# Attention by groups: V in high and low halves, two heads' turned probabilities split, scaled by GpSimd, query tile by query tile

## What is computed

```
g_logits                                   # 3 gates (sigmoid) per head
q: 16 heads of 64;  kc,vc, ks,vs, kw,vw: 4 groups of 64 (one group serves 4 heads)
p_c = masked_softmax(q . compress(kc) * scale)          # 31 compressed keys
o_c = p_c @ compress(vc)
o_s = masked_softmax(q . ks * scale, causal) @ vs        # 512 keys
o_w = masked_softmax(q . kw * scale, causal) @ vw        # 512 keys
o   = o_c * gates[0] + o_s * gates[1] + o_w * gates[2]
return o.reshape(S, 1024) @ w_out
```

## Time and profile before

| | |
|---|---|
| time, median of 3 runs | 1523.73 us (1522.63 to 1525.72) |
| profiled execution: time, span | 1524.09 us, 1522.3 us |
| busy: PE, PEld, DVE, ACT, POOL | 1468.9, 1221.6, 718.9, 716.8, 677.4 us |
| PE busy, share of the span | 96% |
| mean granted TensorE clock | 0.991 |
| attention groups of layer 1 | about 775 to 1050 us |

### The profile page before, as it was taken

One profiled execution on the slowest core, in us unless ns is written; L12 is line 12 of the kernel. 1 busy time (PEld: TensorE's weight loads), 2 busy tenths in 40 slices (PEclk: granted clock), 3 DMA queues, 4 the chain that ended last, 5 costly groups with the idle time before them and its releaser, 6 DMA issues.

```text
span 1522.3 us, 23455 instructions
## 1 busy us (share of the span) xinstructions
PE 1468.9 (96%) x7566; PEld 1221.6 (80%) x7566; DVE 718.9 (47%) x1256; ACT 716.8 (47%) x1305; POOL 677.4 (44%) x970
## 2 busy tenths in 40 slices
PE   6999978999999999999999999999999999999998
PEld 5877757888888888877978787878888888888886
DVE  5477772643434300246466767674644444410053
ACT  5245543654444423357365656464744444423262
POOL 4634434365656555364420202111465656555452
PEclk9999998999999999999999999999999999999999
DMA  5321111223232333242510101010132222332221
GB/s 201 121 70 56 55 42 56 94 100 106 87 106 87 106 102 97 70 135 84 167 44 15 56 1 55 14 41 21 66 136 96 96 96 96 96 97 98 97 97 56
DMA packets 37131, 126.22 MB, mean 83 GB/s; under 512 B 6096, under 2 KB 6864, under 8 KB 36816
## 3 DMA queue, kind: packets, MB, share of 16 engines
q1 hardware_dynamic: 31824, 115.88, 22.9%
q10 hardware_dynamic: 5248, 9.55, 1.8%
HBM read 123.32 MB, written 2.10 MB: 82 GB/s over the span
## 4 chain that ended last, share of the span: by engine, by line
PE 58%; issue 17%; POOL 16%; DVE 5%; ACT 4%; POOLq 0%; ACTq 0%; DVEq 0%
PE banks_a L1204 22%; POOL w_lo L297 15%; PE banks_b L1213 9%; PE banks_a L1213 8%; PE banks_a L1576 4%; PE banks_b L1204 4%; PE banks_a L1181 4%; PE banks_b L1548 2%; PE banks_b L1368 2%; DVE nm L940 1%; PE banks_a L1387 1%; PE banks_a L1467 1%; ACT w_hi L358 1%; ACT y L361 1%; PE banks_b L1551 0%
## 5 line engine op out<-in xcount | busy, mean ns | idle before, releaser
L297 POOL TENSOR_TENSOR w_lo<-w_raw,w_hi 128x256 fp32r<-128x256 f32 x852 | 648.0, 793 | 767.0 <-ACT w_hi L358 766.9
L358 ACT ACTIVATE w_hi<-w_raw 128x1024 fp32r<-128x1024 f32 x213 | 225.6, 1061 | 284.1 <-PE banks_b L1213 137.5
L1204 PE MATMUL banks_a<-nT_hi,w_hi 128*128 128x512 f32 (+1 forms) x968 | 344.5, 377 | 0.0
L1204 PE MATMUL banks_a<-nT_lo,w_hi 128*128 128x512 f32 (+1 forms) x968 | 342.7, 375 | 0.0
L1204 PE MATMUL banks_a<-nT_hi,w_lo 128*128 128x512 f32 (+1 forms) x968 | 342.2, 375 | 0.0
L1204 PEld LDWEIGHTS banks_a<-nT_hi,w_hi 128*128 128x128 f32 x968 | 174.6, 190 | 32.0
L1204 PEld LDWEIGHTS banks_a<-nT_hi,w_lo 128*128 128x128 f32 x968 | 173.7, 189 | 32.1
L1204 PEld LDWEIGHTS banks_a<-nT_lo,w_hi 128*128 128x128 f32 x968 | 173.8, 189 | 31.3
L846 DVE SCALAR_TENSOR_TENSOR y<-banks_a,conv,y 128x511 f32<-128x511 f32 x88 | 66.0, 750 | 218.2 <-ACT y L459 217.6
L459 ACT ACTIVATE y<-banks_a,conv 128x512 f32<-128x512 f32 x88 | 68.6, 780 | 207.6 <-PE banks_a L1204 207.5
L940 DVE TENSOR_REDUCE nm<-banks_b 128x2 f32<-128x256 f32 (+2 forms) x96 | 79.2, 825 | 27.1 <-PE banks_b L1371 14.5
(11 more groups left out here) (256 smaller groups left out, 2400.6 us busy)
## 6 DMA issues: line engine op xcount, KB each, us to landing
w_raw<-in_w SPq DMA_DIRECT2D x213, 512.0 KB, 3.3
g_pre<-in_gains ACTq DMA_DIRECT2D x6, 512.0 KB, 5.1
x<-in_x SPq DMA_DIRECT2D x4, 512.0 KB, 9.6
g_post<-in_gains ACTq DMA_DIRECT2D x4, 512.0 KB, 7.6
out<-x SPq DMA_DIRECT2D x4, 512.0 KB, 2.6
pe_raw<-in_pT ACTq DMA_DIRECT2D x2, 512.0 KB, 6.0
w1k<-in_w ACTq DMA_DIRECT2D x1, 1024.0 KB, 4.9
w1v<-in_w ACTq DMA_DIRECT2D x1, 1024.0 KB, 6.9
```

The lines of the kernel that those rows point to most:

```text
L297: pool.tensor_tensor(w_lo[slot][:, cols], w_raw[k % RAW][:, cols], w_hi[slot][:, cols].bitcast(F32), ALU.subtract).then_inc(S["w_lo_done"], 1)
L358: act.activation(w_hi[u % RING][:, :], w_raw[u % RAW][:, :], ACT.Copy).then_inc(S["w_hi_done"], 1)
L1204: m = pe.matmul(bank[:, cols], w[:, k * P:(k + 1) * P], r[:, k, cols], start=(k, pas) == (0, 0), stop=(k, pas) == (KT - 1, 2))
```

## The change

All of it lies in the groups of layer 1.

- **Steps.** `sequence` now runs over head pair m, tile k and branch c. A step holds one branch of two heads j, and steps 0 to 7 of a pair have 1, 1, 4, 4, 2, 2, 3, 3 key blocks. Scores, maxima, exponentials and transposes are as many and as wide as before.
- **Normalising and gates.** After the exponentials of a step VectorE clamps and inverts the row sums (`inverse_sums`), and GpSimd multiplies `gp` in place by the inverse and by the gate (`weigh`): two TENSOR_SCALARs a step. `gturn` waits for them.
- **Chunks.** Turned probabilities are handled in 12 chunks for each pair (24 in a group), of one or two key blocks of both heads, 256 or 512 columns. ScalarE copies a chunk to `gpT_hi`, then VectorE subtracts that into `gpT_lo`.
- **Values.** `Vs` holds V's high and low half side by side as the weights (128 columns); the turned probabilities stream, 256 columns at a time, in `float32r`. Two products for each key block, and the result comes out turned already, with the low half's product in rows 64 to 127. All branches accumulate in A[0] and A[1].
- **End of a pair.** ScalarE copies rows 64 to 127 out (`spill`), VectorE adds them (`fold`); `gturn_o`, `read_branches` and `add_branches` are gone. For the first pair this happens at step 9.
- **Compressed branch.** `Vc` replaces `Vblk`, its low half is made once and copied to three more row blocks; the compressed probabilities are normalised and gated before they are turned, split in high and low, and `cvalues` opens the accumulation (8 products for each pair). VectorE's `blocks_out` is gone.
- TensorE and GpSimd have the four groups written out instead of a loop; GpSimd's `low` of a group's fourth unit is spread behind steps 3 to 6.

```diff
+        sequence = [(m, c, k) for m in range(2) for k in range(TT) for c in range(2)]
+        chunks = [(n, kb, min(2, ORDER[k] + 1 - kb)) for n, (m, c, k) in enumerate(sequence)
+                  for kb in range(0, ORDER[k] + 1, 2)]
+        CHUNKS = len(chunks)
+        chunks_of = [[i for i in range(CHUNKS) if chunks[i][0] == n] for n in range(len(sequence))]
...
+            def weigh(g, n):
+
+                m, c, k = sequence[n]
+                qt = ORDER[k]
+                width = (qt + 1) * P
+                pool.wait_ge(S["gstat_done"], 16 * g + n + 1)
+                for j in range(2):
+                    cols = gp[:, n % DEEP, j, 0:width]
+                    gate = gates[:, qt, bass.ds(12 * g + (3 * (2 * m + j) + 1 + c), 1)]
+                    pool.tensor_scalar(cols, cols, grec[:, n % 4, j:j + 1], gate, ALU.mult, ALU.mult)\
+                        .then_inc(S["gnorm_done"], 1)
...
+                for n in range(len(sequence)):
+                    weigh(g, n)
+                    if 3 <= n < 3 + PARTS:
+                        low(UG + 3, (UG + 3) % RING, UG + 4 * i + 4, (n - 3,))
+            for g in range(GROUPS):
+                group(g, g)
...
+            act.wait_ge(S["vclo_done"], 1)
+            for h in range(1, GHEADS):
+                signal(act.activation(Vc[N_PAD * h:N_PAD * h + N_PAD, :, HEAD:2 * HEAD],
+                                      Vc[0:N_PAD, :, HEAD:2 * HEAD].bitcast(F32), ACT.Copy), "kvc_done", GHEADS + h)
...
+            def spill(pair):
+                act.wait_ge(S["gpv_done"], (CHUNKS // 2) * pair + CHUNKS // 2)
+                for j in range(2):
+                    signal(act.activation(of_half(oT[side(j), :]), of_head(side(1), j), ACT.Copy), "gspill_done",
+                           2 * pair + j + 1)
+
+            def goT_high(pair):
...
+                    signal(act.activation(gp[:, n % DEEP, j, 0:width], B[2 * (n % 2) + j][:, 0:width], ACT.Exp,
+                                          bias=nm[:, n % 4, j:j + 1], accum_out=gsum[:, n % 4, j:j + 1]),
+                           "gprobs_done", 32 * g + (2 * n + j + 1))
+
+                def gpT_high(i):
+                    width = 2 * P * chunks[i][2]
+                    act.wait_ge(S["gT_done"], CHUNKS * g + (i + 1))
+                    if not (first and i < DEEP):
+                        act.wait_ge(S["gpv_done"], CHUNKS * g + (i + 1 - DEEP))
+                    signal(act.activation(gpT_hi[:, i % DEEP, 0:width], A[2 + i % 2][:, 0:width], ACT.Copy),
+                           "gpThi_done", CHUNKS * g + (i + 1))
...
+                signal(act.activation(pcT_hi[:, :], A[3], ACT.Copy), "cpThi_done", g + 1)
...
+                signal(act.activation(Vs[:, :, :, 0:HEAD], A[2].rearrange("p (t c d) -> p t c d", t=TT, c=2), ACT.Copy),
+                       "vshi_done", g + 1)
+                for j in range(2):
+                    gexps(1, j)
+                for n in range(len(sequence)):
+                    for j in range(2):
+                        if j < len(chunks_of[n]):
+                            gpT_high(chunks_of[n][j])
+                        if n + 2 < len(sequence):
+                            gexps(n + 2, j)
+                        if j == 0 and n == 9:
+                            spill(2 * g)
                     if n == 1:
                         w_high(u + 3, i, per)
+                    if n == 10:
+                        goT_high(2 * g)
+                spill(2 * g + 1)
...
+                for j in range(2):
+                    dve.wait_ge(S["gspill_done"], 2 * pair + j + 1)
+                    dve.tensor_tensor(of_half(oT[side(j), :]), of_head(side(0), j), of_half(oT[side(j), :]), ALU.add)                        .then_inc(S["gfold_done"], 1)
...
+                def gpT_low(i):
+                    width = 2 * P * chunks[i][2]
+                    dve.wait_ge(S["gpThi_done"], CHUNKS * g + (i + 1))
+                    signal(dve.tensor_tensor(gpT_lo[:, i % DEEP, 0:width], A[2 + i % 2][:, 0:width],
+                                             gpT_hi[:, i % DEEP, 0:width].bitcast(F32), ALU.subtract), "gpTlo_done",
+                           CHUNKS * g + (i + 1))
+
+                def inverse_sums(n):
+                    dve.wait_ge(S["gprobs_done"], 32 * g + (2 * n + 2))
+                    link(dve.tensor_scalar(grec[:, n % 4, :], gsum[:, n % 4, :], 1e-30, None, ALU.max))
+                    signal(dve.reciprocal(grec[:, n % 4, :], grec[:, n % 4, :]), "gstat_done", 16 * g + n + 1)
...
+                    if n == 0 and first:
+                        dve.wait_ge(S["kvc_done"], GHEADS)
+                        signal(dve.tensor_tensor(Vc[0:N_PAD, :, HEAD:2 * HEAD],
+                                                 A[2][0:N_PAD, P:P + GROUPS * HEAD].rearrange("p (g n) -> p g n", g=GROUPS),
+                                                 Vc[0:N_PAD, :, 0:HEAD].bitcast(F32), ALU.subtract), "vclo_done", 1)
...
+                signal(dve.tensor_tensor(pc[:, :, :, :].rearrange(flat), pc[:, :, :, :].rearrange(flat),
+                                         cst[:, 2, :].unsqueeze(2).broadcast_to([P, TT * GHEADS, N_PAD]), ALU.mult),
+                       "cp_done", g + 1)
+                dve.wait_ge(S["cpThi_done"], g + 1)
+                signal(dve.tensor_tensor(pcT_lo[:, :], A[3], pcT_hi[:, :].bitcast(F32), ALU.subtract), "cpTlo_done", g + 1)
+                dve.wait_ge(S["vshi_done"], g + 1)
+                signal(dve.tensor_tensor(Vs[:, :, :, HEAD:2 * HEAD], A[2].rearrange("p (t c d) -> p t c d", t=TT, c=2),
+                                         Vs[:, :, :, 0:HEAD].bitcast(F32), ALU.subtract), "vslo_done", g + 1)
+                gmaxima(1)
+                inverse_sums(0)
+                gmaxima(2)
+                inverse_sums(1)
+                for n in range(len(sequence)):
+                    for j in range(2):
+                        if j < len(chunks_of[n]):
+                            gpT_low(chunks_of[n][j])
+                        if j == 0:
+                            if n == 9:
+                                fold(2 * g)
+                            if n + DEEP < len(sequence):
+                                gmaxima(n + DEEP)
+                    if n + 2 < len(sequence):
+                        inverse_sums(n + 2)
+                    if n == 11:
+                        goT_low(2 * g)
+                fold(2 * g + 1)
...
-                    mm = transpose(A[2 + m][:, tok(t)], opair[:, m, tok(t)])
-                mm.then_inc(S["goT_done"], 1)
...
+                    pe.wait_ge(S["cpTlo_done"], g + 1)
+                    if m:
+                        pe.wait_ge(S["gfold_done"], 4 * g + 2)
+                    for turn in range(2):
+                        for j in range(2):
+                            t = turn ^ j
+                            bank = A[t].rearrange("p (t j q) -> p j t q", t=2, j=2)
+                            cols = slice(2 * P * t, 2 * P * t + 2 * P)
+                            rows = slice(N_PAD * (2 * m + j), N_PAD * (2 * m + j) + N_PAD)
+                            pe.matmul(bank[:, j], Vc[rows, g, :], pcT_hi[rows, cols], start=turn == 0,
+                                      stop=False)
+                            ins = pe.matmul(bank[0:HEAD, j], Vc[rows, g, 0:HEAD], pcT_lo[rows, cols], start=False,
+                                            stop=False)
+                            ins.then_inc(S["cv_done"], 1)
+                        if turn == 0:
+                            pe.wait_ge(S["cv_done"], 8 * g + 4 * m + 2)
...
+                    elif n > 1:
+                        pe.wait_ge(S["gprobs_done"], 32 * g + 2 * (n - 1))
...
+                def gturn(i):
+                    n, kb0, kbs = chunks[i]
+                    if kb0 == 0:
+                        pe.wait_ge(S["gnorm_done"], 32 * g + 2 * n + 2)
+                    if i >= 2:
+                        pe.wait_ge(S["gpTlo_done"], CHUNKS * g + (i - 1))
+                    else:
+                        pe.wait_ge(S[("vslo_done", "cpTlo_done")[i]], g + 1)
+                    for kb in range(kbs):
+                        for j in range(2):
+                            m = transpose(A[2 + i % 2][:, (2 * kb + j) * P:(2 * kb + j + 1) * P],
+                                          gp[:, n % DEEP, j, (kb0 + kb) * P:(kb0 + kb + 1) * P])
+                    m.then_inc(S["gT_done"], 1)
+
+                def gvalues(i):
...
+                    pe.wait_ge(S["gpTlo_done"], CHUNKS * g + (i + 1))
+                    cols = slice(2 * P * (qt % 2), 2 * P * (qt % 2) + 2 * P)
+                    for kb in range(kbs):
+                        at = slice(2 * P * kb, 2 * P * kb + 2 * P)
+                        pe.matmul(A[qt // 2][0:HEAD, cols], Vs[:, kb0 + kb, c, 0:HEAD], gpT_lo[:, i % DEEP, at],
+                                  start=False, stop=False)
```

(22 more changed lines are left out.)

278 lines of the change are left out of this document (80 added, 198 removed).

## The result

The changed kernel takes 1579.8 us, median of 4 runs (1574.4 to 1588.2), against 1524.0 us before: 1.037 times as long, 95% interval 1.032 to 1.042. Slower, as forecast, but by 56 us and not by 31: the forecast of 1555 us was 25 us short, and its range (1534 to 1578) was missed by 2 us.

A forecast was written before the change was run, and what follows sets the result against it. TensorE was taken to set the pace of the steps. Per group, start +3.8, steps and end +2.8, head transposes -0.8: four groups +23.4, first group +1.6, sum +25, clock +6, giving 1555 us (range 1534 to 1578).

The forecast's parts named there:

- TensorE's own saving: TensorE's work in a group's sixteen steps falls from 41.1 to about 32.4 us; little of it could be seen.
- Rival 2: TensorE remains the limit in the steps and its saving comes through: -5.6 us a group, 1503 us; chance 0.06.
- rival 4: Handover and later start hide better; steps go at ScalarE's pace, 38 us with the end, no difference; chance 0.04.
- GpSimd's W: GpSimd's two scaling instructions a step, in the chain before the transposes: 1.66, 1.34, 1.02, 0.70 us for 512 to 128 columns.
- Rival 1: GpSimd's scaling is cheap, near its smallest instruction, and the clock stays at full speed: 1538 to 1545 us; chance 0.10.
- The start: At a group's start, normalising before turning delays the first transposes of `gp` by 3.8 us; +1.6 more in the first group.
- the sum: Start, steps with end, and dropped head transposes over four groups, plus the first group's extra: +25 us before the clock.
- The sign named for it: About 5 us from the compressed probabilities' transposes to the first of `gp`, where it was 2.4.
- Spill: First pair's handover in step 9, on ScalarE and VectorE: 2.3 us by step 11, some 1.2 reaching the end.
- The steps' walk: Step-by-step chain through ScalarE, VectorE, GpSimd and TensorE: last products end at 44.4 us; steps and end +2.8 a group.
- The clock: TensorE's clock falls in each group, little of it showing: +1.5 us a group (0 to 4), +6 in all.
- Rival 3: Clock stays at 1.2 GHz through the steps and TensorE bounds again: about 10 us more a group, 1595; chance 0.08.

The follow-up runs named there:

- e1: Changed kernel plus three float32r products of 512 columns, their result overwritten, ahead of every step's first transposes of probabilities: 1565.7 us.
- e12: As e1, but `spill` and `fold` of the first pair work on one query column of 128: 1559.3 us.
- e7: Changed kernel without GpSimd's scaling of the probabilities and with three added products a step: 1551.9 us.
- e5: Changed kernel plus one added product of 512 columns ahead of each step's first transposes: 1574.2 us.
- e9: Changed kernel with ScalarE's exponentials of step n+2 ahead of step n's copies, and VectorE's inverse ahead of the low parts: 1609.3 us.
- e13: Changed kernel with TensorE's scores of step n+3 ahead of step n's transposes, and VectorE's maxima of them ahead of step n's low parts: 1649.0 us.
- e11: As e9, plus a reordered group start (V handled ahead of the compressed probabilities) and two added products a step: 1608.5 us.
- e14: As e13, plus three added products a step: 1680.2 us.
- e16: As e13, plus a reordered group start (V handled ahead of the compressed probabilities) and two added products a step: 1657.0 us.

## Why the prediction was right in sign and short in size

- **TensorE's own saving: right.** In e1 TensorE is busy 43.16 us in the steps; less 48 products of 0.23 that is 32.1, the forecast said 32.4. It bought nothing, as said. Rival 2 is out: steps and end are 48.3 at full clock where it needed under 38.6. So is rival 4, which had them at 38.
- **GpSimd's W: right.** 0.77, 0.66, 0.61, 0.45 us against 0.83, 0.67, 0.51, 0.35 assumed: 9.9 us a pair's eight steps against 9.4. Rival 1 is out. The Trainium skill (GPSIMD Engine Reference, 4.1 Engine selection) says that one-input operations run roughly at line rate. Worked out as an estimate, at one column a cycle and the page's 1.2 GHz, that is 0.43 us for 512 columns, and with the 0.20 us of the earlier trace rows the forecast's 0.63. The rows agree with it on the growth from 128 to 512 columns (0.32 us for 384 columns) and not on the fixed part, which is some 0.34 us and not 0.20.
- **The start: right.** +17.3 us against 16.8 in the sum (4 x 3.8 + 1.6). The sign named for it came too, 876.44 to 881.29, 4.85 us.
- **Spill: right in kind, small.** 1.2 us a group was put on it; e12 measured 0.5 to 0.6 in the two groups with equal clock (some 1.6 a group in the medians, clock included), the wait of `cvalues` is 0.49 us.
- **The steps' walk: the second term that was mis-sized, 2 to 3 us a group short.** Start of the first copy of each step, counted from that of step 0, in e1's second group against the walk:

| step | 2 | 4 | 6 | 8 | 10 | 12 | 14 | end |
|---|---|---|---|---|---|---|---|---|
| walk | 5.4 | 11.5 | 16.7 | 21.3 | 27.7 | 34.7 | 40.7 | 44.4 |
| e1, clock 1.00 | 5.5 | 12.2 | 17.2 | 22.9 | 29.1 | 36.3 | 42.9 | 48.0 |
| after, 0.76 | 5.9 | 14.6 | 20.8 | 26.5 | 33.1 | 42.0 | 49.7 | 55.3 |

e1's steps took 3.4 to 3.7 us more than the walk's 44.9 (44.4 and the 0.5 ahead of S(0)) in three groups and 5.3 in the first, where the clock was 0.93; an estimated 1.0 to 1.6 of it is the added products' own time (e7, e5), the rest is the walk's. That it came so near is in part luck. Without W the walk had 39 to 42 us, and e7 has 46.6 at full clock, 45 or more with the products' time taken off: the walk put too much on the way through GpSimd (measured 1.7 us in the steps) and too little on the rest, and the two errors offset. The runs don't divide the rest further.
- **The clock: the step that failed.** The forecast wrote "I expect it to fall in each group, and with ScalarE setting the pace little of it to show: +1.5 us a group", +6 in all. The fall came (0.80, 0.76, 0.76, 0.81 in the four groups' steps), the conclusion was wrong. ScalarE doesn't set the pace: e7's steps are 46.6 us at full clock against its 38. The pace is a ring, in which TensorE's transposes and scores stand between GpSimd and ScalarE and between ScalarE and VectorE's maxima, and scores start 0.43 us apart at 1.2 GHz and not 0.23. Holding the clock gave 14 us net (e1), 22 us against the profiled execution's steps (217.4 to 195.4), and with the products' own price of 4 to 6 us taken off, it is an estimated 18 to 20 for the medians, where the sum had 6. Rival 3, at 1595, had 46 (1595 less the 1549 of the sum without clock); its condition (clock down through the steps) was met for about half of the time, but its mechanism wasn't: TensorE doesn't bound again, it still waits 13 us a group for GpSimd. The Trainium skill (TensorE: Matmul & The Clock Gate, part 1) tells of two levels, 1.2 and 2.4 GHz; the windows at 0.50 and 1.00 and the spacing of 0.43 and 0.23 us agree.

The account: 56 us measured, forecast as 25 + 6. By the runs the clock is some 18 to 20 and the rest 36 to 38. Of that rest the starts are 17, the projections -3, and the steps some 20 to 22 (26.0 in e1 less the products' 4 to 6), where the walk had 11; some 2 us stay unplaced. So of the 25 us by which the forecast was short, an estimated 12 to 14 are the clock's price and 9 to 11 the walk. The range's upper end (1577 for the forecast) was the dearest W with 4 us a group for the clock; W came in a little above its middle value, and nothing in the range allowed for the walk itself being short, or for a clock dearer than 4 us a group.

What stays open: how the remainder of the steps at full clock divides between ScalarE, VectorE and TensorE. Changes of order that I expected to shorten it (e9, e13) lengthened it, so my picture of which step is next in the ring was wrong twice. In e1's table the last stretch stands out: from step 14 on it takes 5.1 us where the walk had 3.7. For the scores, an emptier bank, which would be the direct test, doesn't exist (A and B use all eight) and wasn't tried.

## What to carry to other kernels

When work is taken off the engine that sets the pace and put into a chain that returns to it, price that engine's part of the chain at both levels of its clock: here the waits that the change created lowered it. Filling such a wait with products whose result is overwritten is a cheap probe, and here gave back 14 of 56 us; it did so only ahead of an instruction that waited anyway (e1), and cost time in e11, e14 and e16. Before moving an instruction ahead in an engine's queue, ask which buffer it needs and who frees it, since everything behind it inherits that wait.
